# SwiGLU gate and up products by seven half products per pair of weight tiles, on one Trainium2 core

## The reference, cut to what matters

```python
def _rmsnorm(x, gain):
    y = x32 * lax.rsqrt(jnp.mean(x32 * x32, axis=-1, keepdims=True) + NORM_EPS)
    return (y * gain).astype(x.dtype)

def _swiglu(x, w_gate, w_up, w_down):                 # D_MODEL 1024, D_FF 2816 = 22 tiles of 128
    hid = jax.nn.silu(jnp.einsum('bsd,df->bsf', x, w_gate)) * jnp.einsum('bsd,df->bsf', x, w_up)
    return jnp.einsum('bsf,fd->bsd', hid, w_down)

for l in range(DEPTH):                                # DEPTH 2
    h = h + 0.5 * _swiglu(_rmsnorm(h, ffn1_norm[l]), ffn1_w_gate[l], ffn1_w_up[l], ffn1_w_down[l])
    h = h + _hybrid_mixer(_rmsnorm(h, mix_norm[l]), ...)
    h = h + 0.5 * _swiglu(_rmsnorm(h, ffn2_norm[l]), ffn2_w_gate[l], ffn2_w_up[l], ffn2_w_down[l])
```

## Time and profile before

| | us |
|---|---|
| median of 3 runs | 3267.9 (3267.48 to 3269.05) |
| the profiled execution | 3268.05 |
| its span, first to last instruction | 3266.2 |
| TensorE busy in the span | 3197.2 |
| DVE busy | 1734.2 |
| ACT busy | 1266.8 |

### The profile page before, as it was taken

The page is one execution under the profiler, slowest core; times in us unless marked ns, Lnnn a source line. Parts: engine busy times, 40 slices in busy tenths (PEclk is TensorE's granted clock), DMA queues, the critical chain, the costliest instruction groups (busy, mean ns, idle before and its releaser), DMA issues.

```text
span 3266.2 us, 38220 instructions
## 1 busy us (share of the span) xinstructions
PE 3197.2 (98%) x14998; PEld 2631.4 (81%) x14998; DVE 1734.2 (53%) x2530; ACT 1266.8 (39%) x1778; POOL 70.5 (2%) x136
## 2 busy tenths in 40 slices
PE   8999999999999999999999999999999999999998
PEld 7888876788888888888678888888888888888887
DVE  5443465764443444336575544357666687454433
ACT  4222335453222322223555322236445576332222
POOL 0000000100000000000010000000000000000000
PEclk9999999999999999999999999999999999999999
DMA  4333322123333333332211333333332233333331
GB/s 154 97 96 95 95 87 66 42 68 100 97 94 97 97 97 97 95 100 87 69 52 43 109 98 95 94 104 94 103 91 83 86 91 101 109 97 97 97 93 63
DMA packets 101825, 296.46 MB, mean 91 GB/s; under 512 B 15328, under 2 KB 26336, under 8 KB 101648
## 3 DMA queue, kind: packets, MB, share of 16 engines
q1 hardware_dynamic: 96048, 278.96, 28.5%
q0 software_dynamic: 5312, 14.02, 1.6%
...
...
## 4 chain that ended last, share of the span: by engine, by line
PE 86%; DVE 6%; ACT 5%; issue 2%; DMA 1%; POOL 0%; ACTq 0%; DVEq 0%; SPq 0%
PE ps L798 26%; PE ps L800 26%; PE ps L799 26%; PE ps L807 2%; ACT wh L1367 1%; DVE mf L2117 1%; DVE wl L1930 1%; PE ps L812 1%; ACT L1358 1%; PE ps L1259 1%; PE ps L1106 1%; PE ps L1139 1%; PE ps L1255 0%; PE ps L1189 0%; ACT mf L1856 0%
## 5 line engine op out<-in xcount | busy, mean ns | idle before, releaser
L1367 ACT ACTIVATE wh<-raw 128x1024 fp32r<-128x1024 f32 (+3 forms) x581 | 566.5, 977 | 1564.8 <-PE ps L800 1564.3
L798 PE MATMUL ps<-hnh,wh 128*128 128x512 f32 x2712 | 1070.9, 395 | 4.2 <-DVE wl L1930 1.7
L800 PE MATMUL ps<-hnh,wl 128*128 128x512 f32 x2712 | 1057.6, 390 | 0.0
L799 PE MATMUL ps<-hnl,wh 128*128 128x512 f32 x2712 | 1057.5, 390 | 0.0
L1930 DVE TENSOR_TENSOR wl<-raw,wh 128x1024 fp32r<-128x1024 f32 (+3 forms) x581 | 652.0, 1122 | 573.0 <-ACT wh L1367 570.2
L798 PEld LDWEIGHTS ps<-hnh,wh 128*128 128x128 f32 x2712 | 510.8, 188 | 116.8 <-issue 13.4
L800 PEld LDWEIGHTS ps<-hnh,wl 128*128 128x128 f32 x2712 | 510.2, 188 | 107.3
L799 PEld LDWEIGHTS ps<-hnl,wh 128*128 128x128 f32 x2712 | 511.1, 188 | 105.6 <-issue 2.2
L798 PE MATMUL ps<-mr,wh 128*128 128x512 f32 x1300 | 509.2, 392 | 1.0 <-DVE mr L2422 0.5
L800 PE MATMUL ps<-mr,wl 128*128 128x512 f32 x1300 | 506.2, 389 | 0.0
L799 PE MATMUL ps<-mr,wh 128*128 128x512 f32 x1300 | 505.8, 389 | 0.0
...
## 6 DMA issues: line engine op xcount, KB each, us to landing
...
```

The costliest lines, as they stand in the source:

```text
L798: self.e.matmul(out, ah, bh, start=start, stop=False, skip_group_check=shared)
L799: self.e.matmul(out, ah, bl, start=False, stop=False, skip_group_check=shared)
L800: m = self.e.matmul(out, al, bh, start=False, stop=stop, skip_group_check=shared)
L1367: self.e.activation(k.spl[u % NSPL][0][:, 0:n], k.raw[u % NRAW][:, 0:n], ACT.Copy).then_inc(k.w_hi, 1)
```

## The change

Pairs 1 to 7 of the eleven pairs of tiles (tiles 2 to 15) are made in another way, for gate and for up, in all five FFNs. The weights of two tiles are a matrix of 2 by 2 blocks: A11 and A12 are blocks 0 to 3 and 4 to 7 of the first tile, A21 and A22 those of the second. The input is 2 by 2 too: B11 and B12 are `hn[0..3]` for tokens 0 to 255 and 256 to 511, B21 and B22 are `hn[4..7]`. The result comes from seven products of four blocks by 256 tokens each, in Winograd's form of Strassen's method, instead of eight.

The sums of the weights are made by DVE in the raw buffers (`sums_of`): S3 = A11 + A21, S1 = A21 + A22, S2 = A11 + S1, S4 = A12 + S2, with signs in the operands. Two tiles now are four units: the first tile (1024 columns), S3 (512), S2 and S4 (1024), S1 and A22 (1024). The sums of the token halves (`halves`, nine steps on DVE and four on ACT, four operands of 1024 columns) are made from `h` once in an FFN, beside pair 0 at a pace of 0.6; what is left of them is made by `until` before pair 1. PSUM banks are passed on by ACT copies from bank to bank between the half products (`between`), since TensorE goes on adding to them. DVE takes the results in halves (`after`). `ready_banks` makes four matmuls per FFN that mark the banks as written. The multiplication by `rs` moves from the up product to the sum of the down product (`add_h`). Loads stay 512 KB each; which `wh` and `wl` a unit has comes from a list (`spl_of`).

```diff
+SEVEN = {p: (True,) for p in range(1, 8)}
+PLAIN, OF_3, OF_24, OF_1 = range(4)
+A1, E3, B2, A12, C1, B22, C4 = range(7)
...
+W_B, W_C, W_E = (5, 2), (6, 7), (3, 4)
...
+        self.f, halves = f, self.halves(f)
+        self.pace = F_PACE
...
+            if seven and i % 2 == 0:
+                if i == 2 * min(SEVEN):
+                    self.until(halves)
+                    self.pace = 0.0
+                    self.give_back()
+                    self.ready_banks()
...
+                self.seven_products(f, i, None)
...
+    def seven_products(self, f, i, hid):
+        self.begin_product(None)
+        a = self.free[0]
+        for n in range(7):
+            self.half_product(n, a)
+            self.between(n, a, i, hid)
+            if n == A1:
+                self.end_pair()
+            if n in (E3, A12, B22, C4):
+                if n == A12:
+                    self.made()
+                self.u += 1
+                self.split_ahead(n)
+            self.after(n, a, f, i, hid)
...
+    def ready_banks(self):
+
+        k = self.k
+        self.wait_ge(*k.rs_v.at(self.rs_n(), "rows"))
+        for b in W_B + W_C:
+            self.e.matmul(k.ps[b][:, 0:256], k.hn[0][0][:, 0:128], k.hn[0][0][:, 0:256], start=True, stop=True)
...
+        unit, at, b = ((0, 0, a), (1, 0, W_E[x]), (2, 0, W_B[x]), (0, 4, a), (3, 0, W_C[x]), (3, 4, W_B[x]), (2, 4, W_C[x]))[n]
+        self.wait_ge(k.w_hi, u0 + unit + 1)
+        self.wait_ge(k.w_lo, u0 + unit + 1)
+        if n == E3:
+            if w >= 2:
+                self.wait_ge(*k.se_a.at(w - 2, "e"))
+            self.wait_ge(*k.ft_v.at(self.f, "l3"))
+        elif n == B2:
+            self.wait_ge(*k.se_a.at(w, "b"))
+            self.wait_ge(*k.ft_v.at(self.f, "l2"))
+        elif n == C1:
+            self.wait_ge(*k.se_a.at(w, "c"))
+            self.wait_ge(*k.ft_v.at(self.f, "l1"))
+        elif n == B22:
+            self.wait_ge(*k.ft_v.at(self.f, "l4"))
+        elif n == C4:
+            self.wait_ge(*k.se_a.at(w, "s"))
+        wh, wl = [t[:, :].rearrange("p (k c) -> p k c", c=128) for t in k.spl[k.spl_of[u0 + unit]]]
...
+    def between(self, n, a, i, hid):
+        k, w = self.k, self.w
+        x = w % 2
+        if n == A1:
+            self.wait_ge(*k.se_p.at(w, "a1"))
+            if w >= 2:
+                self.wait_ge(*k.se_v.at(w - 2, "c21"))
+            self.e.activation(k.ps[W_B[x]][:, 0:256], k.ps[a][:, 0:256], ACT.Copy).then_inc(*k.se_a.up(w, "b"))
+        elif n == B2:
+            self.wait_ge(*k.se_p.at(w, "b2"))
+            if w >= 2:
+                self.wait_ge(*k.se_v.at(w - 2, "c1"))
+            self.e.activation(k.ps[W_C[x]][:, 0:256], k.ps[W_B[x]][:, 0:256], ACT.Copy).then_inc(*k.se_a.up(w, "c"))
+        elif n == A12:
+            self.wait_ge(k.unit_done, self.u)
+            if w:
+                self.wait_ge(*k.se_v.at(w - 1, "c21"))
+            self.e.activation(k.third[:, :], k.ps[W_E[x]][:, 0:256], ACT.Copy, scale=-1.0).then_inc(*k.se_a.up(w, "e"))
+        elif n == C1:
+            self.wait_ge(*k.se_p.at(w, "c1"))
+            if hid is None:
+                self.wait_ge(*k.ffn_v.at(NH * self.f + i - 1, "lo"))
+            elif self.up_w is not None:
+                self.wait_ge(*k.se_v.at(self.up_w, "c2"))
+            to = k.tmp(1 if hid is None else 2)
+            self.e.activation(to[:, 256:512], k.ps[W_C[x]][:, 0:256], ACT.Copy).then_inc(*k.se_a.up(w, "s"))
+            if self.put_off is not None:
+                was, self.put_off = self.put_off, None
+                self.split(was)
...
+    def sums_of(self, u):
+        k, e, m = self.k, self.e, self.adds
+        one, two = k.half_raw(u - 1)[0], k.half_raw(u)[0]
+        a11, a12, a21, a22 = one[:, 0:512], one[:, 512:1024], two[:, 0:512], two[:, 512:1024]
+        e.tensor_tensor(k.tmp(3)[:, :], a11, a21, ALU.add).then_inc(*k.add_v.up(m, "s3"))
+        e.tensor_tensor(a21, a21, a22, ALU.add).then_inc(*k.add_v.up(m, "s1"))
+        self.wait_ge(*k.add_v.at(m, "s1"))
+        e.tensor_tensor(a11, a11, a21, ALU.add).then_inc(*k.add_v.up(m, "s2"))
+        self.wait_ge(*k.add_v.at(m, "s2"))
+        e.tensor_tensor(a12, a12, a11, ALU.add).then_inc(*k.add_v.up(m, "s4"))
...
+    def after(self, n, a, f, i, hid):
+        k, e, w = self.k, self.e, self.w
+        x = w % 2
+        g0, g1, rs = k.tmp(0), k.tmp(1), k.rs
+        to = k.tmp(1 if hid is None else 2)
+        if n == A12:
+            self.wait_ge(k.unit_done, self.u)
+            if hid is None:
+                self.wait_ge(*k.ffn_v.at(NH * f + i - 2, "lo"))
+                e.tensor_tensor(g0[:, 0:256], k.ps[a][:, 0:256], rs[:, 0:256], ALU.mult).then_inc(k.took, 1)
+            else:
+                self.wait_ge(*k.ffn_s.at(NH * f + i, "silu"))
+                e.tensor_tensor(g0[:, 0:256], g0[:, 0:256], k.ps[a][:, 0:256], ALU.mult).then_inc(k.took, 1)
+            self.flush()
+        elif n == C1:
+            self.wait_ge(*k.se_a.at(w, "s"))
+            e.scalar_tensor_tensor(out=to[:, 256:512], in0=to[:, 256:512], scalar=-1.0, in1=k.third[:, :],
+                                   op0=ALU.mult, op1=ALU.add).then_inc(*k.se_v.up(w, "c22"))
+        elif n == B22:
+            self.wait_ge(k.unit_done, self.u)
+            if hid is None:
+                self.wait_ge(*k.ffn_v.at(NH * f + i - 1, "lo"))
+            e.scalar_tensor_tensor(out=to[:, 0:256], in0=k.ps[W_B[x]][:, 0:256], scalar=-1.0, in1=k.third[:, :],
+                                   op0=ALU.mult, op1=ALU.add).then_inc(*k.se_v.up(w, "c21"))
+            self.wait_ge(*k.se_v.at(w, "c21"))
+            if hid is None:
+                e.tensor_tensor(g1[:, :], g1[:, :], rs[:, :], ALU.mult).then_inc(*k.se_v.up(w, "c2"))
+            else:
+                self.wait_ge(*k.ffn_s.at(NH * f + i + 1, "silu"))
+                e.tensor_tensor(g1[:, :], g1[:, :], to[:, :], ALU.mult).then_inc(*k.se_v.up(w, "c2"))
+            self.flush()
+        elif n == C4:
+            self.wait_ge(k.unit_done, self.u)
+            if hid is None:
+                e.tensor_tensor(g0[:, 256:512], k.ps[W_C[x]][:, 0:256], rs[:, 256:512], ALU.mult).then_inc(*k.se_v.up(w, "c1"))
+            else:
+                e.tensor_tensor(g0[:, 256:512], g0[:, 256:512], k.ps[W_C[x]][:, 0:256], ALU.mult).then_inc(*k.se_v.up(w, "c1"))
+            self.flush()
...
+            self.e.scalar_tensor_tensor(out=g[:, :], in0=b[:, :], scalar=scale, in1=k.rs[:, :],
+                                        op0=ALU.mult, op1=ALU.mult).then_inc(*k.ffn_h.up(8 * f + i, "rs"))
+            self.wait_ge(*k.ffn_h.at(8 * f + i, "rs"))
+            self.e.tensor_tensor(k.h[i][:, :], k.h[i][:, :], g[:, :], ALU.add).then_inc(k.took, 1)
...
-        e.tensor_tensor(g[:, :], g[:, :], k.rs[:, :], ALU.mult).then_inc(*k.ffn_v.up(n, "up"))
...
+    def paired(w, i):
+        out.append((w[i], 1024, PLAIN))
+        out.append((w[i + 1], 512, OF_3))
+        out.append((None, 1024, OF_24))
+        out.append((None, 1024, OF_1))
```

More of the change, by code:

```diff
@@ L130, in __init__ @@
         self.units, self.marks = plan_units(ins)
+        self.loads, self.raw_of, self.spl_of = [], [], []
+        released = []
+        for u, (src, n, part) in enumerate(self.units):
+            if src is not None:
+                self.loads.append([src, n if part == PLAIN else 1024, u])
+            back = 1 if part == OF_24 else 0
+            self.raw_of.append(len(self.loads) - 1 - back)
+            self.loads[-1 - back][2] = u
+            self.spl_of.append(u if u < NSPL else self.spl_of[released[u - NSPL]])
+            if part in (OF_3, OF_1):
+                released.insert(u - 1, u)
+            else:
+                released.append(u)
         sem = lambda n: ctx.enter_context(nc.semaphore(n))
@@ L465, in norm_ready, with add_h_all @@
         self.run_late()
-    def add_h_all(self, xs, ready, scale, gain):
+    def add_h_all(self, xs, ready, scale, gain, f=None):
         self.hn_last = self.u
@@ L479, in ffn @@
         hid = [k.pair(2 * i, 2 * i + 1) for i in range(NH)]
+        self.f, halves = f, self.halves(f)
+        self.pace = F_PACE
         for i in range(NH):
+            seven = SEVEN.get(i // 2)
             if f == 0 and i == 0:
@@ L490, in ffn @@
+            if seven and seven[0]:
+                if i % 2 == 0:
+                    self.seven_products(f, i, hid[i:i + 2])
+                    if i // 2 + 1 not in SEVEN:
+                        self.end_pair()
+                continue
+            if not seven:
+                self.product_h()
+                if i == 0:
+                    self.norm_ready()
+                    self.work.append(halves)
+                self.ffn_gate(f, i)
             self.product_h()
             self.ffn_up(f, i, hid[i])
-        self.add_h_all(hid, lambda i: (k.ffn_a.at(NH * f + i, "hi"), k.ffn_v.at(NH * f + i, "lo")), scale, gain)
+        self.banks_back()
@@ new lines, in ffn, with halves @@
```

(52 more changed lines are left out.)

208 lines of the change are left out of this document (165 added, 43 removed).

## The result

| | before | after |
|---|---|---|
| median, 4 runs each | 3268.5 us (3267.5 to 3269.9) | 3243.1 us (3242.3 to 3245.7) |
| ratio | | 0.9923, 95% interval 0.9906 to 0.9941 |
| span of the profiled execution | 3266.2 us | 3240.8 us |

One of the four runs of experiment 5 took 13911.6 us at a mean granted clock of 0.216, and the medians in this text leave it out.

A forecast was written before the change was run, and what follows sets the result against it. Gate and up stages were taken as bound by TensorE's matmul count and spacing. -56.0 + 20.8 + 10.9 + 1.4 + 6.5 = -16.4 from 3268.05 gave 3252 us, range 3236 to 3276.

The forecast's parts named there:

- Gain on TensorE: Gate and up pairs in five FFNs: 10.08 us instead of 10.88 for each of 70, -56.0 us.
- Rivals 4 and 5: Half-product starts pay 0.08 us for waits, 3280 us, chance 0.05; 256-column matmuls over 0.12 us apart, given nothing.
- No stall in the steady state: Gate and up pairs: DVE's loops of 9.9 us fit TensorE's 10.08, margin 0.14 us, so no steady stall.
- Rivals 1 and 3: DVE loops 0.1 to 0.3 us over TensorE's, centre 3266, chance 0.17; DVE instructions don't overlap, 3300, chance 0.10.
- Entries in FFNs 1 to 4: Start of pair 1, where the token halves' sums are made: stalls of 5.2 us, four times, +20.8 us.
- E3: Half product at the entry to pair 1: stall of 2.3 us in FFN 1, start at 54.5 in FFN 0.
- A1: Half product at the entry to pair 1: stall of 0.95 us in FFN 1 until gate tile 1's bank is free.
- B2: Half product at the entry to pair 1: stall of 1.1 us in FFN 1, behind ACT's copy of a bank.
- Entry in FFN 0: Start of pair 1, with only two products between it and the first pair: stall of +10.9 us.
- Ends: One more DVE instruction before h: +0.7 us at the second block's start and +0.7 at the last tile, +1.4.
- Clock: Slower granted clock after the entry stalls: +1.7 us in FFN 0, 1.2 in each other FFN, +6.5 in all.
- rival 2: Entries to pair 1 cost half of the stalls' 31.7 us and of the clock's: 3233 us, chance 0.13.

The follow-up runs named there:

- experiment 5: Changed kernel with half products for pairs 2 to 7 only and the side-work counter set to 0.8 at both mixers and the second block: 3210.0 us.
- Experiment 4: Changed kernel with six more 16-column DVE instructions, which nobody reads, before each S3: 3265.2 us.
- experiment 2: Kernel before, with only the side-work counter set to 0.8, 0.6 and 0.8 at the mixers and second block, as in the changed kernel: 3259.5 us.
- experiment 3: Changed kernel with seven half products for pairs 2 to 7 only, side-work counter at the mixers and second block kept at 0.8, 0.6, 0.8: 3216.1 us.
- experiment 1: Changed kernel with the side-work counter set to the earlier kernel's 0.0, 0.6 and 0.2 at the mixers and second block: 3260.9 us.

## Why the prediction was right, and where not

The time lay in the stated range, but 9 us below the forecast, at the edge of the forecast's own range of 3243 to 3261. That it stayed inside is partly luck. The sum lacks a term of some -9 us, which is over half of the -16.4 that it comes to, and the range was not made for such a term. Step by step:

- **Gain on TensorE: right.** With 256 columns, also from one half product to the next:

```profile
803.80 0.28 PE L916 MATMUL ps<-hnh,wh 128*128 128x256 f32 x1
803.92 0.28 PE L917 MATMUL ps<-hnl,wh 128*128 128x256 f32 x1
804.04 0.28 PE L918 MATMUL ps<-hnh,wl 128*128 128x256 f32 x1
804.16 0.28 PE L916 MATMUL ps<-mr,wh 128*128 128x256 f32 x1
```

  That is 0.120 us each, as in the earlier trace rows, and 10.08 us for a pair product. Rivals 4 and 5 fall with it: the start of a half product at 804.16 pays nothing for its waits. By the figure that the prediction quotes from the Trainium skill, "TensorE: Matmul & The Clock Gate", section "Back-to-back issue gap", the distance would be 0.109 us; no row here shows that. The section gives this figure for a single matmul by itself, without its weight load, and not for a stream of pairs of load and matmul, which this kernel has.
- **No stall in the steady state: right.** The loop is 10.08 us. The prediction puts the margin at 0.14 us, though its own terms (6.09 + 3.81 = 9.90) leave 0.18; it is 0.15 to 0.17. Experiment 4 shows that what goes beyond it comes on top of the time. Rivals 1 and 3 fall.
- **Entries in FFNs 1 to 4: right in size.** Laid on FFN 1 of before, gate tile 1 was to be taken by 758.8; less the 5.2 us by which this FFN starts earlier that is 753.6, and it was taken by 752.93 + 0.69 = 753.6. TensorE's waits there, by the rows of FFN 1:

```profile
PE ps L916 <- DVE mr L2276: 2.3, 1, 2.3
PE ps L916 <- DVE mf L2426: 0.9, 1, 0.9
PE ps L916 <- DVE wl L2173: 0.3, 1, 0.3
```

  E3 waits 2.3 us as forecast, A1 0.9 where 0.95 were forecast, and B2 0.3 where 1.1 were. B2 waits for DVE's rest (L2173) there, and not for ACT's copy (L1559) as the prediction has it. In FFNs 3 and 4 B2 waits 2.2 us, because the second L2276 stands behind L2433 there (shown above). The prediction read the order for FFN 1 alone.
- **Entry in FFN 0: right.** E3 was to start at 54.5:

```profile
49.36 1.19 PE L999 MATMUL ps<-hnh 128*128 128x256 f32 x4 [6.16 <-DVE mf L2433]
...
55.45 0.55 PE L916 MATMUL ps<-mr,wh 128*128 128x256 f32 x1 [2.34 <-DVE mr L2276]
```

  It started at 55.45, and 0.9 of the 0.95 us is the later start of the FFN. Most of the wait stands before L999, not before E3, since `give_back`, ahead of L999, waits until the up tile has been taken out of its bank (L2433). The prediction doesn't have this wait. It costs nothing, because E3 has to wait for L2276 in any case.
- **Ends: half right.** The last h is 0.71 us later:

```profile
3226.01 0.68 DVE L2406 SCALAR_TENSOR_TENSOR mf<-ps,mf 128x512 f32<-128x512 f32 x1
3226.72 0.69 DVE L2409 TENSOR_TENSOR h<-h,mf 128x512 f32<-128x512 f32 x1
```

  At the start of the second block the 0.7 became 0.1. In the kernel before it took 2168.20 + 4.62 = 2172.82 from the last sum to the last block's matmul, in the changed one 2150.88 + 4.72 = 2155.60. Before, DVE had waited 0.53 us for ACT between the two, and the new instruction (L2409) lies in that gap.
- **Clock: right in kind, too small in size.** The clock's part in the five FFNs is 10.2 us where 6.5 were put. It is 5.1 in FFN 0, where 1.7 were put, 1.7 in FFNs 1, 2 and 4, where 1.2 were, and nothing in FFN 3. Partly it lies under waits, so it doesn't add up with them. FFNs 3 and 4 have the same waits of 5.4 us; FFN 4 has a fall of the clock and FFN 3 none, and FFN 4 is 1.5 us longer.
- **The step that failed** is one that isn't there. The sum costs what is added and moved in the FFNs, and takes the mixers' times as given, without a reason; its only term outside the FFNs is that of the ends. But the diff sets `self.pace = F_PACE`, and the counter that it feeds outlives the FFN. In the first mixer and the second block the same work came in another order. That is worth some -9 us: -10.5 over the three stretches with the clock's part, and -9.1 in experiment 2, which changes nothing else. Comparing the order of both kernels past the FFNs would have shown that the mixers differ, though not which way.

The stretches add up to the whole: +0.9 (start) +1.1 -17.7 (FFNs) -7.2 +2.5 -5.7 (mixers) +0.7 (end) = -25.4 us. A term of -9 would bring the prediction's -16.4 to the same number, because the rest nearly cancels: +0.9 at the start and +1.2 in the FFNs, against -1.7 of the clock's in the mixers and -0.6 at the start of the second block. The time alone would have misled: a result 9 us under the forecast looks like half of rival 2 (entries cheaper, 3233 us). The stretches and experiment 3 show that the entries cost what was forecast.

What stays open: why 0.9 us more pass before the first gate tile (33.0 to 35.6 over all profiles, with a fall of the clock in some of them), why the clock fell more often in experiment 1, and what exactly makes 0.2 a middling remainder.
